# Hyena's filter network moved into retention's first pass, and its filters and spectra computed as products of rounded parts

## The reference, cut to what matters

```python
def hyena_filters(length, w1, b1, f1, w2, b2, f2, w3):
    ...                                              # z: (length, 33), a constant table
    hid = jnp.sin(f1 * (z @ w1 + b1))                # (length, 64)
    hid = jnp.sin(f2 * (hid @ w2 + b2))
    h = (hid @ w3).reshape(length, HY_ORDER, 2, HY_W)
    return (h * jnp.exp(-t * deltas)[:, None, None, :]).astype(F32)

def two_sided_fftconv(u, h_f, h_b):
    kern = jnp.concatenate([h_f, jnp.zeros_like(h_f[:1]), h_b[1:][::-1]], axis=0)
    kf = jnp.fft.rfft(kern, axis=0)                  # the spectrum that the kernel keeps in KS
    ...

def retention_scan(q, k, v, log_g, s0):              # chunks of 128 rows, forward and backward
    scores = jnp.einsum('bhncd,bhnsd->bhncs', qc, kc) * dmat[None, :, None]
    y_intra = jnp.einsum('bhncs,bhnse->bhnce', scores, vc)
    kv = jnp.einsum('bhnsd,bhnse->nbhde', kc * k_decay[...], vc)
    def step(s, kv_n):
        return g_chunk * s + kv_n, s
    ...
```

## Time and profile before

| | us |
|---|---|
| median of three timed runs | 4486.12 |
| profiled execution, its own time | 4480.53 |
| span of its trace | 4478.8 |
| retention stage, first DMA to next stage's first DMA | 2395.3 to 2530.65 |
| filter stage, the same | 2530.65 to 2737.25 |
| busy PE, DVE, ACT, POOL over the whole span | 4027.4, 2604.2, 1482.7, 619.8 |
| mean granted TensorE clock | 0.940 of full speed |

### The profile page before, as it was taken

How to read it: one execution, slowest core, us unless ns; L and a number is a source line. 1 busy time by engine, 2 the same in 40 slices (tenths; PEclk the granted TensorE clock), 3 DMA queues, 4 the chain that set the end, 5 groups by cost and what they waited for, 6 DMA issues and landing times. The chain is left out here.

```text
span 4478.8 us, 71317 instructions
## 1 busy us (share of the span) xinstructions
PE 4027.4 (90%) x27486; PEld 3117.5 (70%) x27486; DVE 2604.2 (58%) x4923; ACT 1482.7 (33%) x3061; POOL 619.8 (14%) x811
## 2 busy tenths in 40 slices
PE   7999999768999989699997696999869999899988
PEld 5877776557888877588776443888757778765647
DVE  5567776667344348734666623777755325465746
ACT  4223232744222235412433301334434311143433
POOL 1111101000000000022111301000110014332320
PEclk9999999889999999899998778999879999999999
DMA  6544432543111145546664113444434335453334
GB/s 210 187 151 139 162 128 101 186 156 99 47 47 47 37 132 160 163 154 213 247 232 150 56 69 122 115 115 124 127 93 151 136 132 187 171 158 97 97 104 154
DMA packets 421988, 599.56 MB, mean 134 GB/s; under 512 B 166703, under 2 KB 279811, under 8 KB 419045
## 3 DMA queue, kind: packets, MB, share of 16 engines
q1 hardware_dynamic: 369037, 417.99, 30.4%
q0 software_dynamic: 51840, 177.16, 10.6%
q10 hardware_dynamic: 792, 0.13, 0.0%
HBM read 430.45 MB, written 164.71 MB: 133 GB/s over the span
## 5 line engine op out<-in xcount | busy, mean ns | idle before, releaser
L154 PE MATMUL g_in_g_acc<-g_in_g_whi,g_in_hi 128*128 128x512 f32 (+1 forms) x832 | 328.2, 394 | 0.6 <-DVE g_in_lo L1432 0.4
L155 PE MATMUL g_in_g_acc<-g_in_g_wlo,g_in_hi 128*128 128x512 f32 (+1 forms) x832 | 318.6, 383 | 0.0
L156 PE MATMUL g_in_g_acc<-g_in_g_whi,g_in_lo 128*128 128x512 f32 (+1 forms) x832 | 318.3, 383 | 0.0
L154 PE MATMUL g_even_g_acc<-g_even_g_whi,h_hi 128*128 128x512 f32 (+1 forms) x720 | 278.4, 387 | 25.6 <-DVE g_even_g_wlo L138 13.5
L155 PE MATMUL g_even_g_acc<-g_even_g_wlo,h_hi 128*128 128x512 f32 (+1 forms) x720 | 274.7, 382 | 0.0
L156 PE MATMUL g_even_g_acc<-g_even_g_whi,h_lo 128*128 128x512 f32 (+1 forms) x720 | 274.7, 382 | 0.0
L1677 DVE SCALAR_TENSOR_TENSOR rows<-up_acc,up_taps,rows 128x1023 f32<-128x1023 f32 x88 | 112.9, 1282 | 270.7 <-ACT rows L1652 263.4
L154 PE MATMUL g_odd_g_acc<-g_odd_g_whi,h_hi 128*128 128x512 f32 x544 | 215.5, 396 | 19.9 <-DVE g_odd_g_wlo L138 14.1
L1601 PE MATMUL up_acc<-h_hi,up_w_hi 128*128 128x512 f32 x704 | 220.6, 391 | 13.1 <-DVE up_w_lo L1691 11.1
L1601 PE MATMUL up_acc<-h_lo,up_w_hi 128*128 128x512 f32 x704 | 220.3, 390 | 0.0
L1601 PE MATMUL up_acc<-h_hi,up_w_lo 128*128 128x512 f32 x704 | 220.0, 390 | 0.0
(11 more groups left out here) (652 smaller groups left out, 9451.3 us busy)
## 6 DMA issues: line engine op xcount, KB each, us to landing
rest<-in_w_down SPq DMA_DIRECT2D x66, 512.0 KB, 3.5
g_in_g_raw<-in_w_in SPq DMA_DIRECT2D x96, 256.0 KB, 3.8
P<-g_in_g_o POOLq DMA_DIRECT2D x96, 256.0 KB, 2.9
g_in_m_w<-in_ada_w SPq DMA_DIRECT2D x24, 1024.0 KB, 5.5
up_w_buf<-in_w_up SPq DMA_DIRECT2D x42, 512.0 KB
U<-g_even_g_o POOLq DMA_DIRECT2D x80, 256.0 KB, 3.0
g_odd_x<-U3p SPq DMA_DIRECT2D x24, 768.0 KB, 7.0
g_in_m_w<-in_w_ada SPq DMA_DIRECT2D x16, 1024.0 KB, 6.3
```

The source lines that it names most:

```text
L154: pe.matmul(bank[:, :wd], hi[:, k, tt], w_h, start=k == 0, stop=False)
L155: pe.matmul(bank[:, :wd], hi[:, k, tt], w_l, start=False, stop=False)
L156: op = pe.matmul(bank[:, :wd], lo[:, k, tt], w_h, start=False, stop=k == KC - 1)
```

## The change

Four things are done.

1. The network leaves the filter stage and goes into the first pass of retention, in pieces of 256 columns: 4 for the first layer, 4 for the second. In round t DVE forms angle t (one operation of 64x256), POOL takes off the whole turns (`pool_reduced`, 11 operations with a drain behind each), ACT takes the sine of piece t-2, and PE multiplies pieces of the second layer by `w2`. The result goes through a DRAM tensor `HID`. The seven small loads for it stand at the head of POOL's stream.
2. The filters become two rounded products of one call: 128 rows that hold the high part of `hid` over its low part against the high part of `w3`, then 64 rows against its low part.
3. The spectra become three rounded products for each float32 product. The high parts are made by ACT, the low parts by POOL (and by DVE for some tiles of the first block and for the table).
4. The filters of the next column block are computed between the spectra of the current one; the list `order()` gives the sequence on every engine.

```diff
+def pool_reduced(pool, out, ang, turns, whole):
+    pool.tensor_scalar(turns, ang, 1.0 / TWO_PI, None, ALU.mult)
+    pool.drain()
+    pool.tensor_scalar(turns, turns, ROUND, None, ALU.add)
+    pool.drain()
+    pool.tensor_scalar(turns, turns, ROUND, None, ALU.subtract)
+    pool.drain()
+    for n, turn in enumerate((PI_1, PI_2, PI_3)):
+        pool.tensor_scalar(whole, turns, -turn, None, ALU.mult)
+        pool.drain()
+        pool.tensor_tensor(ang, ang, whole, ALU.add)
+        pool.drain()
+    pool.tensor_scalar(ang, ang, PI_LIM, None, ALU.min)
+    pool.drain()
+    pool.tensor_scalar(out, ang, -PI_LIM, None, ALU.max)
+    pool.drain()
...
 def retention_stage(...):                      # in_order, at the end of round t of the first pass
+            if 0 <= t - 2 < 8:
+                part("sine", t - 2)
+            if t == -1:
+                part("net", 0)
+            if 0 <= t - 3 < 4:
+                part("net", t - 2)
+            if 0 <= t < 8:
+                part("angle", t)
...
+                if what == "angle":            # POOL
+                    pool.wait_ge(s.ang, t + 1)
+                    if t >= 2:
+                        pool.wait_ge(s.sine, t - 1)
+                    pool_reduced(pool, arg[:, two(t)], ang[:, two(t)], turns, whole)
+                    pool.sem_inc(s.arg, 1)
...
+                if what == "sine":             # ACT
+                    act.wait_ge(s.arg, t + 1)
+                    act.activation(hid[:, c], arg[:, two(t)], ACT.Sin).then_inc(s.sine, 1)
...
+                if what == "angle":            # DVE
+                    dve.wait_ge(s.h_mm, t - 2 if n else 1)
+                    if t >= 2:
+                        dve.wait_ge(s.arg, t - 1)
+                    dve.tensor_scalar(ang[:, two(t)], ..., ALU.add, ALU.mult).then_inc(s.ang, 1)
...
 def hyena_filter_stage(...):
-                for n in range(4):             # PE, filters
-                    pe.matmul(acc[:, k % 2 * 4 + n], tokens, w3p[:, n * HYW:(n + 1) * HYW], start=True, stop=True).then_inc(s.w3_mm, 1)
-                for r in range(2):             # PE, spectra
-                    for k in range(NT // 2):
-                        op = pe.matmul(acc[:, 2 * (u % BANKS) + r], w[:, c % 2, r * (NT // 2) + k, n, :], z[:, o, r, k, n, :], ...)
+    def order():
+        yield "table", (0, 0)
+        yield "pair", 0
+        yield "split", (0, 0)
+        for k in range(1, NT):
+            yield "chunk", (0, k)
+            yield "split", (0, k)
+            if k % 2 == 0:
+                yield "low", (0, k - 1)
+        yield "low", (0, NT - 1)
+        yield "table", (0, 1)
+        for u in range(BLOCKS * FCH):          # 4 x 4
+            b, c = divmod(u, FCH)
+            if u:
+                yield "out", divmod(u - 1, FCH)
+            if b + 1 < BLOCKS:
+                for k in range(3 * c, min(3 * c + 3, NT)):
+                    if k:
+                        yield "chunk", (b + 1, k)
+                    elif b % 2:
+                        yield "pair", (b + 1) // 2
+                    yield "split", (b + 1, k)
+            if u + 2 < 2 * FCH:
+                yield "table", divmod(u + 2, FCH)
+            yield "spec", (b, c)
+        yield "out", (BLOCKS - 1, FCH - 1)
...
+            def rows_of(b, k):                 # PE, filters: one call
+                pe.matmul(fil[i % 4][:], rows_[:, 2 * k2 + r, :], m_hi[:, cols], start=True, stop=False)
+                pe.matmul(fil[i % 4][:], rows_[halves[0], 2 * k2 + r, :], m_lo[:, cols], start=False, stop=True).then_inc(s.w3_mm, 1)
...
+                    for r in range(2):         # PE, "spec"
+                        for k2 in range(K2):
+                            k = r * K2 + k2
+                            pe.matmul(acc[u % 2][r][:], th[:, n, c, k, :], zh[:, b % 2, k], ...)
+                            pe.matmul(acc[u % 2][r][:], th[:, n, c, k, :], zl[:, b % 2, k], ...)
+                            op = pe.matmul(acc[u % 2][r][:], tl[:, n, c, k, :], zh[:, b % 2, k], ...)
...
+                if what == "split" and not by_vector(*at):     # POOL
+                    pool.wait_ge(s.z_hi, NT * b + k + 1)
+                    pool.tensor_tensor(zl[:, b % 2, k], zsrc, zh[:, b % 2, k], ALU.subtract).then_inc(s.z_lo, 1)
...
+                if what == "chunk":            # DVE: waits until the low part two chunks back is out, then
+                    scale(b, k, 2 + j % 2)     # zt = product * decay
```

More of the change, by code:

```diff
@@ L2396, in retention_stage @@
         y = sb("y", [P, 2, HN, HD])
+        feats = sb("feats", [33, SEQ])
+        w1s = sb("w1s", [33, 64])
+        w2s = sb("w2s", [64, 64])
+        f_cols = sb("f_cols", [64, 4])
+        ang, turns, whole = (y[0:64].rearrange("p a h d -> p (a h d)")[:, n:m] for n, m in ((0, 512), (512, 768), (768, 1024)))
+        arg = sq[0:64].rearrange("p h d -> p (h d)")
+        two = lambda t: slice(t % 2 * 256, (t % 2 + 1) * 256)
+        hid = work[0:64, 0:SEQ]
+        net_out = lambda q: po[q % 2][0:64].rearrange("p b t -> p (b t)")[:, q // 2 * 256:(q // 2 + 1) * 256]
+        first_out = lambda q: po[q // 2][0:64].rearrange("p b t -> p (b t)")[:, q % 2 * 256:(q % 2 + 1) * 256]
         pkv = [ps(f"pkv{i}", [P, 4, P]) for i in range(2)]
@@ L2412, in part @@
                     sp.dma_start(qk[:, t % 4], U2[t * P:(t + 1) * P, 0:1024]).then_inc(qk_in[t % 4], DMA)
+                if what == "out" and t == 0:
+                    sp.wait_ge(s.sine, 8)
+                    sp.dma_start(HID, hid).then_inc(s.hid_kept, DMA)
                 if what == "store":
@@ L2497, in part @@
                     op.then_inc(s.scores, 1)
+                if what == "net" and t == 0:
+                    pe.wait_ge(s.f_const, 7 * DMA)
+                    for hf in range(2):
+                        op = pe.matmul(po[hf][0:64].rearrange("p b t -> p (b t)"), w1s[:], feats[:, hf * 512:(hf + 1) * 512], start=True, stop=True)
+                    op.then_inc(s.h_mm, 1)
+                if what == "net" and t:
+                    pe.wait_ge(s.sine, t)
+                    pe.wait_ge(s.ang, (2, 4, 5, 6)[t - 1])
+                    pe.matmul(net_out(t - 1), w2s[:], hid[:, (t - 1) * 256:t * 256], start=True, stop=True).then_inc(s.h_mm, 1)
                 if what == "out":
@@ L2702, in _ @@
+            in_order(part)
             for n in range(2):
[L2703 removed]
+                pool.wait_ge((s.ks_even, s.ks_odd)[n], BLOCKS * FCH // 2 * DMA)
         @block.tensor
         def _(pe):
[L2707 to L2715 removed]
@@ new lines, in part @@
+            def part(what, at):
+                if what == "pair":
+                    if at:
+                        dve.wait_ge(s.z_lo, lows(1, 0))
+                    for n in range(2):
+                        scale(2 * at + n, 0, n)
+                    dve.drain()
+                    dve.tensor_tensor(mean[:], zt[0:1, 0], zt[0:1, 1], ALU.add)
+                    dve.drain()
+                    for n in range(2):
+                        dve.tensor_scalar(zt[0:1, n], mean[:], 0.5, None, ALU.mult)
@@ new lines, in _ @@
+            dve.wait_ge(s.w3_in, 2 * DMA)
+            for o in range(2):
+                ahead, back = (w3s[:, (2 * o + n) * HYW:(2 * o + n + 1) * HYW] for n in range(2))
+                dve.tensor_tensor(w3p[:, 2 * o * HYW:(2 * o + 1) * HYW], ahead, back, ALU.add)
+                dve.tensor_tensor(w3p[:, (2 * o + 1) * HYW:(2 * o + 2) * HYW], ahead, back, ALU.subtract)
+            dve.drain()
+            dve.sem_inc(s.paired, 1)
+            dve.wait_ge(s.hid_hi, 2)
+            dve.tensor_tensor(flat_tile(rows_, halves[1]), by_tile(hid, halves[1]), flat_tile(hid_hi, halves[1]), ALU.subtract).then_inc(s.hid_lo, 1)
```

287 lines of the change are left out of this document (170 added, 117 removed).

## The result

| | before | after |
|---|---|---|
| median of 18 runs each | 4489.99 us | 4496.57 us |
| ratio to before, 95% interval | | 1.0022 (1.0014 to 1.003) |
| profiled execution: its time, span | 4480.53, 4478.8 us | 4496.06, 4494.1 us |
| POOL busy over the span | 619.8 us | 748.6 us (17%) |

The change makes the kernel slower by 0.22%. The ratio goes by the means, which differ by 9.7 us, without one run of the kernel before that took 8282.02 us; the medians differ by 6.6. I had forecast a gain of 35 us.

The account below looks back on a forecast made before the run. DVE was taken to pace retention's first pass and PE to bound two thirds of the filter stage. Terms -57 - 11 + 33 = -35 us gave 4445, forecast as 4451 against the median of the runs; range 4429 to 4474.

Parts of the forecast that it names:

- POOL's arithmetic is dear: Rival for retention: a POOL operation of 64x256 costs 1.27 us like the 128x512 addition; time 4520; chance 0.09.
- Retention, POOL: Retention's first pass: 11 POOL operations for each of 8 pieces, one-input ones at 0.40 us, 6.9 a piece; cost 33 us.
- POOL and DVE hinder each other, 13 us: Retention's first pass: POOL loses 0.27 us to each of 50 two-input DVE operations, 13 us.
- the rule's 4463: Retention: by the skill's exclusion rule POOL loses a whole DVE operation of 0.53 each time, 12 us more, time 4463.
- The rest of POOL's chain: Retention's first pass: POOL starts at 2426.7 less 0.5, has nine forward steps of 1.62 us, and ends at 2509.0.
- What stands ahead of the first unit, 31 us: Filter stage: the first unit starts 31 us after the stage instead of 88.1, bounds 25 and 38; gain 57 us.
- Spectra and the other filters, 101.2 us: Filter stage: 430 products at 0.2267 us, with clock start and waits 101.2 against 112.4 us; gain 11.
- Second pass as before: Retention's second pass stays as long as before, 52.7 us.
- Feeding: Rival for the filter stage: PE waits for the splitting, six units cost 2 us more, 12; time 4463; chance 0.15.
- Lower clock: Rival for the filter stage: all 430 products stay at the lower clock, 0.427 us each; time 4534; chance 0.03.
- DVE at 0 because POOL paces: Retention's first pass: eight angles on DVE, 4 us if DVE paced, count 0 because POOL will be later.
- The range: Total time 4429 to 4474 us, leaving one in ten out on each side.

Follow-up runs that it names:

- second_op6: Changed kernel with its 11 POOL operations a piece, each one-input operation given a second arithmetic step that changes nothing: 4465.14 us (one run).
- full_rows5: Changed kernel with the second product of each filter call reading 128 rows, 64 of them zeros, instead of 64: 4493.31 us (one run).
- nine operations: Changed kernel with POOL's piece as 9 operations of two steps or two inputs, z loaded by SP, filter products on 128 rows: 4446.43 and 4448.31 us.
- drain_gaps7: The version with nine operations plus a DVE drain behind each scaled key and each of the four rotation products: 4447.65 us, ratio to before 0.9916.
- pool_fused5: Changed kernel with POOL taking off the whole turns in 8 operations a piece, several fused, instead of 11: 4466.43 us (one run).
- turns_on_dve5: Changed kernel with the whole turns taken off by DVE, 7 operations a piece, in place of POOL's 11: 4474.53 us, ratio 0.997.

## Why the prediction was wrong

Retention was to lose and the filter stage to win, and so they did, with POOL pacing the first pass; but retention lost twice what I had, and with it the sign of the sum was wrong. Most of what came was the rival *POOL's arithmetic is dear*. I had worked out that 0.40 us more per operation turns the gain into nothing; 64 of the 88 operations cost 0.44 more and the other 24 nothing more, 28.4 us of the 35. The rest of the gain went to the wait on DVE and to the filter products.

- *"Retention, POOL", one-input operations at 0.40.* The step that failed. I took the copy's row as the nearest, and it is a different form; 0.843 - 0.40 for 64 operations is 28.4 us. Shown by `second_op6`, which takes 25.2 us off with nothing else changed.
- *POOL and DVE hinder each other, 13 us.* Measured in the changed kernel: POOL's operations from 2424.6 to 2545.5 take 102.2 us where their clean times make 83.2, so 19.0. Three operations that had to wait out a run of DVE are 10.2 of it. The other 8.8 are losses of mostly 0.20 to 0.42 each, near the 0.27 to 0.42 of the earlier trace rows. The page of the Trainium skill that I set aside there, "SBUF — State Buffer", "Who interferes with whom", says that issue order decides who blocks. The three waits agree with it in kind and go beyond an instruction: six in a row kept POOL out. Such a wait happened in the first rounds and once later, so one whole DVE operation for each of POOL's, the rule's 4463, would have named neither the place nor the size.
- *The rest of POOL's chain.* It began 1.6 us earlier than I had it; the wait for `z` was 1.9 inside the first piece; the drains' gaps were 16.8 in all for 14.8. With 28.4 and 6.0 that is 36.7, and less 0.2 in the `forward` steps and additions POOL's pass ended at 2545.5 instead of 2509.0. The stage itself began 3.3 later in this trace, so 33.2 of the 36.5 are longer work, which is 66.3 less 33.
- *What stands ahead of the first unit, 31 us.* 32.1, and 56.0 gained for my 57: right in size, in part by luck. The list of steps puts eleven filter calls there and 21 behind, not nine and 23, and PE, not the loop of DVE, ACT and POOL, sets the pace. Its 22 products run back to back at a granted clock of 0.50, 0.72 us apart, from 2616.4 to 2632.3:

```profile
2616.38 0.76 PE L2850 MATMUL hy_fil<-hy_m_hi,hy_rows 128*128 128x512 f32 x1 [25.72 <-DVE hy_m_lo L2975]
2617.07 0.79 PE L2851 MATMUL hy_fil<-hy_m_lo,hy_rows 64*128 64x512 f32 x1
```

- *Spectra and the other filters, 101.2 us.* 106.9. I priced the filter products, 64-row and 128-row in turn, as products of 128 rows. `full_rows5` takes 8.1 us off that stretch (42 such products at 0.2 make 8.4). Without them the term would have been 98.8, 2.4 less than mine: 0.9 for four products that I had there and that run ahead of the first unit, the rest my allowances for clock and waits.
- *Second pass as before.* 53.7 against 52.7: right. *Feeding*: PE is busy for 101.3 of 101.3 us and its list of waits behind 2632 is empty, so no unit waited. *Lower clock*: 1.00 behind the first 6 us. *DVE at 0 because POOL paces*: right in the changed kernel (39.4 us of DVE's waits for POOL); with nine operations DVE has 0.4 us of such a wait left in a round.
- *The range.* It ended at 4474. What came, slower by less than 0.3%, I had given 0.07. I had bounded the one-input operation by 1.27 and written that no row showed it; with an unseen form under 64 instances, the weight of the copy's row was too great. The range hung on it: with 0.40 the kernel takes 4465 (`second_op6`, one run), inside it though 14 above the forecast, and with 0.84 it takes 4497.

## What to carry to other kernels

An operation that no row shows isn't priced by a row of another form, be it of the same width and engine: multiply the bounds by the count first, and if the change lives or dies by that, say so in the chances. Moving work to an idle engine is only free if a piece of it and that engine's own work fit into one round; here a network that took 32.9 us in turn cost 66.3 spread over an idle POOL, and 25.6 once each operation had its cheap form and the load of `z` stood elsewhere. And a wait that is only moved from POOL to DVE wins nothing where both are nearly full, as `drain_gaps7` shows.

## What the runs showed of the hardware

- On POOL, a `tensor_scalar` of 64x256 with one step takes 0.843 us, with multiply and add or min and max 0.395 to 0.40, with subtract and multiply 1.06 (`after`, `second_op6`, `pool_fused5`). On DVE one step takes 0.28 (`turns_on_dve5`).
- A POOL operation that came in at the head of a gapless run of six DVE operations with two SBUF inputs took 3.6 to 4.3 us instead of 0.4 to 0.85; a drain between DVE's operations brought it to 0.67 and lengthened DVE's four from 2.48 to 3.43.
- Products whose weights have 64 and 128 rows in turn start 0.427 us apart at a granted clock of 1.00, and 0.227 with 128 rows each. At 0.50 it is 0.723 and 0.427 (`after`, `full_rows5`).
